# Second attention block: operands of the scores from channel-major projections and DMA instead of operand turns on TensorE

## The reference

```python
h = rmsnorm(x, norm1_g)
z = h @ w_in                     # conv value and gate, q, k, v, f_logit, two branch gates
ya = conformer_conv(a_val, a_gate, ...)
c = cumsum(log_sigmoid(f_logit + fox_bf))            # per head, over the tokens
s = q @ k.T / 8 + c[query] - c[key]                  # 16 heads of 64 channels
ob = softmax(where(key <= query, s, NEG)) @ v
mix = (sigmoid(g_a) * ya + sigmoid(g_b) * (ob @ w_fox_out)) @ w_out
x = x + mix; x = x + peer_ffn(rmsnorm(x, norm2_g)); out = rmsnorm(x, normf_g)
```

## Time and profile before

| quantity | value |
|---|---|
| median of 3 runs (lowest to highest) | 3450.8 us (3449.87 to 3456.03) |
| profiled execution, its own time | 3451.16 us |
| profiled span of the core | 3449.3 us |
| PE busy over the span | 3170.2 us (92%) |
| DVE, ACT, POOL busy | 2685.4 us (78%), 1703.0 us (49%), 753.8 us (22%) |
| granted TensorE clock, mean | 0.984 |

### The profile page before, as it was taken

The page is one execution under the profiler, slowest core; times in us unless marked ns, Lnnn a source line. Parts: engine busy times, 40 slices in busy tenths (PEclk is TensorE's granted clock), DMA queues, the critical chain, the costliest instruction groups (busy, mean ns, idle before and its releaser), DMA issues. The chain is left out here.

```text
span 3449.3 us, 39164 instructions
## 1 busy us (share of the span) xinstructions
PE 3170.2 (92%) x13398; PEld 2167.2 (63%) x13398; DVE 2685.4 (78%) x4212; ACT 1703.0 (49%) x2787; POOL 753.8 (22%) x724
## 2 busy tenths in 40 slices
PE   9999989999999999999999999888888888888876
PEld 7778767777777777767787888444433343444322
DVE  7777689999999999967994745876777777767674
ACT  3245348888888888842234622433333333333332
POOL 0000001100100111110000101444444444444442
PEclk9999999999999999999999999999999999999999
DMA  8422279999999999973233036999999999999998
GB/s 299 139 86 104 76 266 397 416 414 412 413 414 410 412 417 413 412 270 94 90 112 120 1 110 234 416 421 421 421 415 420 416 408 416 413 421 414 421 421 338
DMA packets 202650, 1096.37 MB, mean 318 GB/s; under 512 B 22241, under 2 KB 31865, under 8 KB 87536
## 3 DMA queue, kind: packets, MB, share of 16 engines
q0 software_dynamic: 79680, 553.91, 39.1%
q1 hardware_dynamic: 117069, 523.62, 38.8%
q10 hardware_dynamic: 5760, 17.04, 1.2%
HBM read 1069.64 MB, written 33.03 MB: 320 GB/s over the span
## 5 line engine op out<-in xcount | busy, mean ns | idle before, releaser
L2187 DVE TENSOR_TENSOR moe_w_lo<-ring,moe_w_hi 128x2048 fp32r<-128x2048 f32 x384 | 862.7, 2284 | 34.0 <-ACT moe_w_hi L2034 33.1
L2034 ACT ACTIVATE moe_w_hi<-ring 128x2048 fp32r<-128x2048 f32 x380 | 719.4, 1914 | 112.2 <-DMA ring<-in_exp_w 90.8
L2971 PE MATMUL last_banks<-last_rows_b,ring 128*128 128x512 f32 x1024 | 486.2, 620 | 119.0 <-ACT ring L3033 119.0
L2971 PE MATMUL last_banks<-last_rows_a,ring 128*128 128x512 f32 x1024 | 478.2, 611 | 98.5 <-ACT ring L3033 98.4
L3070 ACT ACTIVATE last_gelu<-last_dot 128x2 f32<-128x2 f32 (+1 forms) x257 | 52.2, 203 | 824.2 <-DVE last_dot L3181 824.1
L2971 PEld LDWEIGHTS last_banks<-last_rows_b,ring 128*128 128x128 f32 x1024 | 191.0, 195 | 390.3 <-issue 197.4
L2850 POOL DMA_INDIRECT last_rows_a<-in_peer_uv,last_ids x256 | 302.6, 1182 | 503.4 <-PE last_banks L2971 318.0
L2971 PEld LDWEIGHTS last_banks<-last_rows_a,ring 128*128 128x128 f32 x1024 | 188.7, 193 | 342.4 <-issue 196.7
L2850 POOL DMA_INDIRECT last_rows_b<-in_peer_uv,last_ids x256 | 282.7, 1104 | 365.6 <-PE last_banks L2971 345.6
L3181 DVE CUSTOM_DVE_ANT_0 last_rows_b<-last_rows_b,ring 128x1024 f32<-128x1024 f32 x128 | 155.7, 1225 | 104.4 <-DMA last_rows_b<-in_peer_uv,last_ids 102.5
L3181 DVE CUSTOM_DVE_ANT_0 last_rows_a<-last_rows_a,ring 128x1024 f32<-128x1024 f32 x128 | 155.5, 1224 | 89.0 <-DMA last_rows_a<-in_peer_uv,last_ids 88.5
(11 more groups left out here) (608 smaller groups left out, 6424.4 us busy)
## 6 DMA issues: line engine op xcount, KB each, us to landing
ring<-in_exp_w SPq DMA_DIRECT2D x384, 1024.0 KB, 10.7
ring<-in_w_in SPq DMA_DIRECT2D x38, 1024.0 KB, 5.4
ring<-in_ada_w SPq DMA_DIRECT2D x12, 1024.0 KB, 11.8
z<-in_ada_w SPq DMA_DIRECT2D x12, 1024.0 KB, 6.1
y_rows<-moe_y ACTq DMA_DIRECT2D x17, 512.0 KB, 7.8
ring<-in_w_out SPq DMA_DIRECT2D x8, 1024.0 KB, 5.1
y_rows<-spare SPq DMA_DIRECT2D x1, 7680.0 KB, 25.4
gate_rows<-conv_held ACTq DMA_DIRECT2D x4, 1024.0 KB, 8.1
```

The lines of the kernel that those rows point to most:

```text
L2034: nc.scalar.activation(w_hi[:, slot, :], env.ring[:, slot, :], ACT.Copy).then_inc(hi_done, 1)
L2187: nc.vector.tensor_tensor(w_lo[:, slot, :], env.ring[:, slot, :], w_hi[:, slot, :].bitcast(F32), ALU.subtract).then_inc(lo_done, 1)
L2971: last = nc.tensor.matmul(sums(t)[:, q, :], diag[:, n % SL], slot(n)[:, D + q * W:D + (q + 1) * W], start=first, stop=final)
```

## The change

Queries and keys of the second attention are projected with the weights as the stationary operand, so `zq` and `zk` hold channels by tokens, chunk i of 128 channels being pair i. The ten small matmuls give the sums as heads by tokens in one tile `sums`. In att2, SP copies by DMA, for each head of a pair, 64 partitions of `zq` and `zk` into `qt` and `kt`, and one row of `sums` into each. The constant rows come from two POOL memsets at the start (-1 in `qt`, +1 in `kt`); the four sum rows of pair 0 are issued after them. From pair 2 on SP waits until all scores of pair i-2 are done. PE waits on `brought` in place of `tq_moved`. The operand turns, their copies on ACT and the preparing copies on POOL are gone from this stage; the first attention keeps them. The result of pair i is written over chunk i of `zq`.

```diff
@@ Tiles.half (multiply passes by_channel on)
+                if by_channel:
+                    lhs, rhs = tuple(a[:, k, t * P:(t + 1) * P] for a in w), tuple(a[:, kk, :] for a in ht)
+                else:
+                    lhs, rhs = tuple(a[:, kk, t * P:(t + 1) * P] for a in ht), tuple(a[:, k, :] for a in w)
+                last = product(self.nc, self.acc[:, t, 0:rhs[0].shape[1]], lhs, rhs, kk == 0, kk == KC - 1)
@@ attention, sync
+            if by_channel:
+                for i, head in enumerate(heads):
+                    if i >= 2:
+                        sp.wait_ge(scored, UNITS * (i - 1))
+                    for u in range(2):
+                        own = slice(u * HD, (u + 1) * HD)
+                        sp.dma_start(qt[0:HD, q_place(i, u), :], zq[own, i, :]).then_inc(brought[i % 2], 16)
+                        sp.dma_start(kt[0:HD, k_place(i, u), :], zk[own, i, :]).then_inc(brought[i % 2], 16)
+                    if i == 0:
+                        sp.wait_ge(ones_set, 2)
+                    for u in range(2):
+                        sp.dma_start(qt[HD:HD + 1, q_place(i, u), :], head.aug_q[u]).then_inc(brought[i % 2], 16)
+                        sp.dma_start(kt[HD + 1:AUG, k_place(i, u), :], head.aug_k[u]).then_inc(brought[i % 2], 16)
@@ attention, gpsimd
+            if by_channel:
+                nc.gpsimd.memset(qt[HD:AUG], -1.0).then_inc(ones_set, 1)
+                nc.gpsimd.memset(kt[HD:AUG], 1.0).then_inc(ones_set, 1)
+                return
@@ attention, tensor: score
                 if t == 0:
-                    pe.wait_ge(tq_moved, moves_before(i))
+                    if by_channel:
+                        pe.wait_ge(brought[i % 2], 8 * 16 * (i // 2 + 1))
+                    else:
+                        pe.wait_ge(tq_moved, moves_before(i))
@@ attention, tensor and scalar (operand and operand_out, for pair 0 and in the steps)
-                if i + 1 < len(heads) and 1 <= n <= len(heads[i + 1].operands):
+                if not by_channel and i + 1 < len(heads) and 1 <= n <= len(heads[i + 1].operands):
                     operand(i + 1, n - 1)
...
@@ conv_and_qkv
-                            nc.tensor.matmul(cps[:, t, :], env.const("ones"), ls[:, s, :], start=(s == 0), stop=False)
-                        last = nc.tensor.matmul(cps[:, t, :], env.const("cum_incl"), ls[:, t, :], start=(t == 0), stop=True)
+                            nc.tensor.matmul(cps[:, t * P:(t + 1) * P], ls[:, s, :], env.const("ones"), start=(s == 0), stop=False)
+                        last = nc.tensor.matmul(cps[:, t * P:(t + 1) * P], ls[:, t, :], env.const("cum_incl"), start=(t == 0), stop=True)
...
-            chain(nc.vector.memset(aug_q[:], 1.0))
-            chain(nc.vector.memset(aug_k[:], 1.0))
...
-                    chain(nc.vector.tensor_copy(aug_q[:, :, :, 0], by_head))
-                    chain(nc.vector.tensor_scalar(aug_k[:, :, :, 1], by_head, -1.0, None, ALU.mult))
+                    chain(nc.vector.tensor_copy(sums[:], cps))
```

More of the change, by code:

```diff
@@ L321, in __init__, with half @@
         self.nc, self.pieces, self.acc, self.done, self.ends = nc, pieces, acc, done, []
-    def half(self, pe, ht, half, freed=None, n_freed=0, after=None, order=range(NT), before={}, arrived=None):
+    def half(self, pe, ht, half, freed=None, n_freed=0, after=None, order=range(NT), before={}, arrived=None, by_channel=False):
         w = self.pieces.take(pe)
@@ L345, in half, with multiply @@
             self.ends.append(self.pieces.takes)
-    def multiply(self, pe, ht, freed=None, n_freed=0):
-        self.half(pe, ht, 0, freed, n_freed)
-        self.half(pe, ht, 1)
+    def multiply(self, pe, ht, freed=None, n_freed=0, by_channel=False):
+        self.half(pe, ht, 0, freed, n_freed, by_channel=by_channel)
+        self.half(pe, ht, 1, by_channel=by_channel)
     def ready(self, eng, j, t):
@@ L913, in __init__, with attention @@
         self.operands = [("q", u) for u in range(len(q))] + [("k", u) for u in range(2 if k else 0)]
-def attention(env, name, zs, heads, fill=None, loads=None, act_between=None, dve_between=None):
+def attention(env, name, zs, heads, fill=None, loads=None, act_between=None, dve_between=None, by_channel=False):
     nc = env.nc
@@ L932, in attention @@
         (prep, tq_turn, tq_moved, scored, maxed, exped, turned, moved, summed, o_free, c_free, chain_s, c_scored, c_sub, c_exp, c_out, masks,
-         zero_set, filled) = (sem(n) for n in (
+         zero_set, filled, ones_set, brought_a, brought_b) = (sem(n) for n in (
             "prep", "tq_turn", "tq_moved", "scored", "maxed", "exped", "turned", "moved", "summed", "o_free", "c_free", "chain", "c_scored", "c_sub",
-            "c_exp", "c_out", "masks", "zero_set", "filled"))
+            "c_exp", "c_out", "masks", "zero_set", "filled", "ones_set", "brought_a", "brought_b"))
+        brought = (brought_a, brought_b)
         block = ctx.enter_context(nc.Block())
@@ L1043, in cmp_value @@
                 last.then_inc(c_out, 1)
-            for m in range(len(heads[0].operands)):
-                operand(0, m)
+            if not by_channel:
+                for m in range(len(heads[0].operands)):
+                    operand(0, m)
             keep_busy(nc, env, sc[:, 0, :], 1)
@@ L1077, in operand_out @@
                 nc.scalar.activation(dst, turn_bank(i, m)[0:AUG, :], ACT.Copy).then_inc(tq_moved, 1)
-            for m in range(len(heads[0].operands)):
-                operand_out(0, m)
+            if not by_channel:
+                for m in range(len(heads[0].operands)):
+                    operand_out(0, m)
             for g in range(STEPS):
@@ L1086, in _ @@
                                      accum_out=rsum[:, i % 2, u, t:t + 1]).then_inc(exped, 1)
-                if i + 1 < len(heads) and 2 <= n <= len(heads[i + 1].operands) + 1:
+                if not by_channel and i + 1 < len(heads) and 2 <= n <= len(heads[i + 1].operands) + 1:
                     operand_out(i + 1, n - 2)
@@ L2424, in _, with conv_and_qkv @@
             keep_busy(nc, env, sums[:, NT % 2, 0, :], 2)
-def conv_and_qkv(env, pieces, ht, zq, zk, zv, conv, glu, sg_dram, aug_q, aug_k, later_loads):
+def conv_and_qkv(env, pieces, ht, zq, zk, zv, conv, glu, sg_dram, sums, later_loads):
     nc, d = env.nc, env.d
@@ L2484, in _ @@
             pe.wait_ge(glu_done, KC - 1)
-            tiles.half(pe, ht, 0, order=(0, 2, 1, 3), before={1: lambda: pe.wait_ge(glu_done, KC)})
-            tiles.half(pe, ht, 1)
+            tiles.half(pe, ht, 0, order=(0, 2, 1, 3), before={1: lambda: pe.wait_ge(glu_done, KC)}, by_channel=True)
+            tiles.half(pe, ht, 1, by_channel=True)
             pe.wait_ge(wf_ok, 2)
@@ L2546, in _ @@
                 next_pieces(2)
-            rows_out(0, lambda t: zq[:, t, 0:W], ACT.Copy, HD ** -0.5)
+            rows_out(0, lambda c: zq[:, c, :], ACT.Copy, HD ** -0.5)
             next_pieces(2)
@@ L2558, in _ @@
             nc.scalar.activation(ls[:], ls[:], ACT.Ln).then_inc(logged, 1)
-            rows_out(3, lambda t: zk[:, t, W:D], ACT.Copy)
+            rows_out(3, lambda c: zk[:, 4 + c, :], ACT.Copy)
             next_pieces(2)
@@ L2679, in second_mixer @@
         sg_dram = [nc.dram_tensor(f"gate_rows{i}", (S, D), F32, kind="Internal").ap() for i in range(2)]
-        aug_q = sb("fox_q", [P, FOX_HEADS, NT, 2]); aug_k = sb("fox_k", [P, FOX_HEADS, NT, 2])
+        sums = sb("fox_sums", [FOX_HEADS, S])
         def first_loads(sp):
@@ L2692, in second_mixer @@
         routed.close()
-        conv_and_qkv(env, pieces, ht, zq, zk, zv, conv, glu, sg_dram, aug_q, aug_k, later_loads)
+        conv_and_qkv(env, pieces, ht, zq, zk, zv, conv, glu, sg_dram, sums, later_loads)
         heads = []
@@ L2696, in second_mixer @@
             pair = [h * HD, (h + 1) * HD]
-            heads.append(Head(pair, pair, pair, [aug_q[:, h], aug_q[:, h + 1]], pair, [aug_k[:, h], aug_k[:, h + 1]]))
+            heads.append(Head(pair, pair, pair, [sums[h:h + 1, :], sums[h + 1:h + 2, :]], pair, [sums[h:h + 1, :], sums[h + 1:h + 2, :]]))
         first_split = [g for g in range(16, 48) if g % 8 >= 4]
@@ L2706, in dve_between @@
                 pieces.split_part(dve, g % 4)
-        attention(env, "att2", (zq, zk, zv), heads, act_between=act_between, dve_between=dve_between)
-        join_and_peer(env, pieces, zq, conv, conv_hi, conv_lo, sga, sg_dram, at)
+        attention(env, "att2", (zq, zk, zv), heads, act_between=act_between, dve_between=dve_between, by_channel=True)
+        o = zq[:].rearrange("p c (t n) -> p t c n", t=NT)
+        join_and_peer(env, pieces, o, conv, conv_hi, conv_lo, sga, sg_dram, at)
 class ByTile:
```

22 lines of the change are left out of this document (11 added, 11 removed).

## The result

The changed kernel takes 3528.55 us (median of 4 runs, 3525.91 to 3555.62) against 3451.03 us of the kernel before beside it (4 runs): ratio 1.024, 95% interval 1.0217 to 1.0264. It is slower by 77.5 us, where I had forecast a gain of 8.3.

The account below looks back on a forecast made before the run. PE was taken to set the pace. 12.8 - 3.1 - 1.2 = 8.5 us off the profiled 3451.16 us gave 3442.7; the median being 0.4 lower, the forecast was 3442.5 us, range 3439 to 3447.5.

Parts of the forecast that it names:

- the clock's: Start of the second attention: PE idles about 6 us, so low clock in pair 0; 1.2 us lost, bounds 0 and 3.1.
- The first rival: Second attention: the clock stays low through the filling of pair 0, another 1.9 us lost, 3444.4 us; chance 0.16.
- Operand turns gone: Second attention: PE drops sixteen turns per pair, full pairs take 11.49 us; 12.8 us saved together.
- DVE next in line: Second attention, pairs with weight splits: DVE is late next but barely fits; nothing taken, upper bound 1.2 us.
- Start of the stage: Second attention: PE waits for memsets and eight DMAs, `score(0)` 3.4 us later; loss 3.1 us, bounds 2.4 and 4.4.
- Projections at zero: Stage before: projections keep count and shape of their matmuls, no cost; the ten small sums zero, bounds -0.5 and +0.5.
- Steady DMAs: Second attention: each pair's eight DMAs start about 12 us before they are needed and take 5.6 us; cost nothing.

Follow-up runs that it names:

- run 2: Not a run label: part of "run 2% slower", said of the by-channel projections against those by rows, 0.233 against 0.229 us per matmul.

## Why the prediction was wrong, point by point

**The step that failed is the clock's.** I wrote: "part of that stretch is waiting anyway, so I take 1.2 us, bounds 0 and 3.1 (two such stretches)". The fall was foreseen; its length was not: the runs show the low clock until the end of the attention. I took the length from the join, and applied it to an attention of which no row of before shows the low level, let alone a recovery. At the join of the kernel before the clock came back at the end of the sixteen transposes without a gap, ahead of the first wide product at 2004.14:

```profile
2004.00:2005.00 1.00, 1.00 (x8) 0.86 (x7) 1.00 (x3) 1.00 (x3) 0.00 (x0) 1.00 1.04 426
```

Even there the price was read a little high: 1.75 us in the earlier trace rows is what the chain kept of the later transposes, the timeline has 1.91, so the low clock cost 1.4 us and not 1.54.

What the fall cost in the attention is measured between the changed kernel and the one with 8 dummy products, stage against stage: 185.7 - 101.1 = 84.6 us. It adds up: six distances of 22.19 instead of 11.50, 64.1; pair 0, 17.38 instead of 9.98, 7.4; pair 7, 27.7 instead of 14.7, 13.0. A fair upper bound was at hand: eight pairs of 11.49 us at half the rate, +92 us. The first rival named the right mechanism, a clock that stays low, but let it end with pair 0 and priced it at 1.9 us; its argument, "once steps follow each other PE is dense", read busy time as what raises the clock. The runs show PE 100% busy at 0.50 as well as at 1.00.

**Operand turns gone: right.** With the clock held, pairs 1 to 6 are 11.50 us apart (forecast 11.49). Against the earlier trace rows that saves 4 x 2.01 + 2 x 1.72 = 11.5 us, and pair 0 went from 11.56 to 9.98 between first scores, 1.6 (forecast 1.3): 13.1 us for 12.8. The 0.3 more is the exponential's table load, which the prediction counted at the start of the stage. That the turns were also the work that restores the clock stood nowhere in the sum.

**DVE next in line: right.** It costs nothing; the pairs with weight splits are 11.50 us apart like the others.

**Start of the stage: the mechanism right, 0.6 us too small.** The first score came 7.47 us behind the stage's start against 3.44 in the earlier trace rows: a delay of 4.0 for 3.4; less 0.3 us of the table load, 3.7 for 3.1, within the bounds of 2.4 to 4.4 (the upper one leaves the table load out; with it a landing of 2.8 us gives 4.1). Issues were 0.63 us apart, not 0.48, and the memsets took 3.70 us, not 3.51. With 8 dummy products the first turn followed the first score by 1.39 us instead of 1.68, the 0.3 us of the table load.

**Projections at zero: wrong by 1.9 us.** I had said that they "keep count and shape", and they do; matmuls start 0.233 us apart instead of 0.229. Why was not tried.

**Steady DMAs: right.** PE waited for a transfer once in the changed kernel's stage, at its start. With the clock at 0.50 that was no test, as each pair took 22.19 us; the version with 8 dummy products is one, and at 11.50 us per pair PE waited once too, 0.33 us at the start.

With the clock held the sum closes: -13.1 + 4.0 + 1.9 = -7.2 us, measured 3444.87 - 3452.6 = -7.7. The forecast of 8.5 would have been about right for a kernel that differs from the changed one by seven dummy products, and in part by luck: the 1.9 us of the projections and the 0.6 too few at the start stand against the 1.2 us that it gave to the clock. (3450.8 - 8.5 is 3442.3; the 3442.5 forecast is that rounded up.)

For the fastest version (2 dummy products, pair 0 brought ahead) the rows explain a stage of 95.7 us instead of 110.2 and 1.9 us lost before it, 12.6 us; the medians differ by 16.8. In its trace the join's sixteen transposes took 1.94 us instead of the 3.29 of the earlier trace rows, another 1.3. The remaining 3 us are open.

## What to carry to other kernels

Removing work from TensorE can remove what holds or restores its clock; before such a change, look for a row in which the remaining work alone raised the clock again, and where there is none, bound the loss by the whole stage at half the rate. Read the granted clock beside the busy share, for a busy share of 100% is shown at both levels. Where a stage starts thin, a dummy product in a wait that exists anyway cost nothing here and held the clock, and bringing the first operands in the stage before made the wait itself short, but by itself did not hold the clock.

## What the runs showed of the hardware

- The same instructions kept either level: 0.50 in 120 us of unbroken work in the changed kernel, 1.00 in 76 us with pair 0 brought ahead and 2 dummy products, according to what came before them. Ten dummy products of 512 columns raised it within the first 6 us (0.72 on the mean there, 1.00 after); sixteen operand turns in each pair raised it some 34 us behind the first score; at the join of the kernel before it rose at the end of sixteen 128x128 transposes without a gap. What about them does so was not separated.
- At the stage's start idle stretches of 1.60, 0.86 and 0.54 us with one dummy product were followed by the fall, 1.60 and 0.54 with two were not. Why 0.87 us of dummy work decides was not settled beyond that.
- The by-channel projections, with the weight as the stationary operand, run 2% slower than by rows, 0.233 against 0.229 us per matmul of the same shape.
- Copies of 2 KB inside SBUF landed 1.7 us after their issue on the median of the changed kernel's stage and 2.0 us at its start, and in 4.5 us where a weight load and eight copies of 128 KB were under way.
